# The 80-row token tile of six projections computed in four column groups of TensorE

## The reference

```python
z = jnp.einsum('btd,de->bte', x, w_in)                 # layer 0, w_in (1024, 3588)
hq, hf, hi, hg, fq, fk, fv, ffg = jnp.split(z, [...], axis=-1)   # 512 columns each, ffg 4
o_hg = rms_norm(o_hg, hg_norm_g).reshape(B, T, HG_VO) * jax.nn.sigmoid(hg)
...
y = jnp.einsum('bte,ed->btd', mixed, w_out)            # layer 0, w_out (1024, 1024)
...
y = jnp.einsum('bte,ed->btd', o.reshape(B, T, MLA_HEADS * MLA_V), w_out)   # layer 1
x = layer_norm(ALPHA * x + y, ...)
f = moe(x, router_w, router_bias, w_gate, w_up, w_down)
```

## Time and profile before

| | us |
|---|---|
| median of 3 runs | 1299.97 |
| fastest and slowest run | 1297.56, 1301.29 |
| the profiled execution | 1298.2 |
| its span, first to last instruction | 1296.4 |
| TensorE busy in it | 1138.6 |
| VectorE, ScalarE, GpSimd busy in it | 568.2, 264.4, 218.1 |
| mean granted TensorE clock | 0.954 of full |

### The profile page before, as it was taken

One profiled execution on the slowest core, in us unless ns is written; L12 is line 12 of the kernel. 1 busy time (PEld: TensorE's weight loads), 2 busy tenths in 40 slices (PEclk: granted clock), 3 DMA queues, 4 the chain that ended last, 5 costly groups with the idle time before them and its releaser, 6 DMA issues.

```text
span 1296.4 us, 16787 instructions
## 1 busy us (share of the span) xinstructions
PE 1138.6 (88%) x6345; PEld 611.3 (47%) x6345; DVE 568.2 (44%) x1252; ACT 264.4 (20%) x624; POOL 218.1 (17%) x382
## 2 busy tenths in 40 slices
PE   8999999999799949999639899999999966999965
PEld 4547777643654323333225455676674422333322
DVE  2079879511634335633265230440352353554334
ACT  1214334311410001111002212332330010111112
POOL 0106445322002101001062300000000110100122
PEclk9999999999999959999959999999999987999988
DMA  8113111361842368999662312000105255999843
GB/s 348 65 40 147 74 66 66 110 215 38 67 173 88 119 274 308 379 422 352 247 210 76 133 44 65 2 1 1 66 1 217 70 223 209 339 398 408 284 141 142
DMA packets 41822, 214.71 MB, mean 166 GB/s; under 512 B 4488, under 2 KB 6088, under 8 KB 32400
## 3 DMA queue, kind: packets, MB, share of 16 engines
q1 hardware_dynamic: 24288, 152.57, 30.3%
q0 software_dynamic: 17168, 60.27, 15.2%
q10 hardware_dynamic: 288, 0.80, 0.2%
HBM read 180.31 MB, written 33.29 MB: 165 GB/s over the span
## 4 chain that ended last, share of the span: by engine, by line
PE 76%; DVE 10%; issue 5%; DMA 4%; ACT 3%; POOL 1%; DVEq 0%; SPq 0%; another core or an unknown queue 0%; ACTq 0%; POOLq 0%
PE pair L1420 12%; PE pair L1324 11%; PE pair L1073 11%; PE pair L1441 6%; PE pair L1084 5%; PE pair L1256 5%; PE pair L1190 4%; PE pair L1518 3%; PE pair L1293 3%; PE pair L1570 2%; DMA arena<-x_rows,ints 2%; PE pair L1406 2%; PE pair L1550 2%; PE pair L1291 2%; PE pair L1114 1%
## 5 line engine op out<-in xcount | busy, mean ns | idle before, releaser
L1073 PE MATMUL pair<-ring,xT 128*128 128x512 f32 (+1 forms) x320 | 138.9, 593 | 0.7 <-DMA ring<-in_even_w_in 0.7
L1420 PE MATMUL pair<-ring,arena 128*32 128x512 f32 x608 | 128.5, 595 | 0.0
L1420 PE MATMUL pair<-arena 128*32 128x512 f32 x736 | 104.1, 622 | 7.7 <-issue 4.2
L1073 PEld LDWEIGHTS pair<-ring,xT 128*128 128x128 f32 (+1 forms) x320 | 57.7, 182 | 76.4 <-issue 75.1
L1190 PE MATMUL pair<-xT,ring 128*128 128x296 f32 x320 | 83.4, 415 | 6.1 <-ACT arena L1609 3.0
L843 POOL TENSOR_SCALAR small<-small 128x1 f32<-128x1 f32 (+3 forms) x45 | 16.3, 363 | 422.5 <-DVE small L2114 362.5
L865 POOL TENSOR_TENSOR arena<-arena 128x128 f32<-128x128 f32 x140 | 56.7, 439 | 154.8 <-PE pair L1116 85.6
L1256 PE MATMUL pair<-arena 128*128 128x264 f32 (+5 forms) x280 | 76.5, 402 | 2.6 <-issue 1.4
L2050 DVE TENSOR_REDUCE small<-pair 128x1 f32<-128x144 f32 (+4 forms) x40 | 22.4, 560 | 120.4 <-PE pair L1261 120.2
L1324 PE MATMUL pair<-ring,mixT 128*128 128x512 f32 (+1 forms) x160 | 72.1, 593 | 1.0 <-issue 1.0
L1324 PE MATMUL pair<-ring,xT 128*128 128x512 f32 (+1 forms) x160 | 71.9, 592 | 0.0
(11 more groups left out here) (357 smaller groups left out, 1914.8 us busy)
## 6 DMA issues: line engine op xcount, KB each, us to landing
arena<-in_moe_w_gate_up SPq DMA_DIRECT2D x14, 2048.0 KB, 9.0
ring<-in_moe_w_gate_up SPq DMA_DIRECT2D x12, 2048.0 KB, 9.6
arena<-in_moe_w_down SPq DMA_DIRECT2D x14, 1024.0 KB, 9.6
y_rows<-arena SPq DMA_DIRECT2D x26, 512.0 KB, 8.5
ring<-in_moe_w_down SPq DMA_DIRECT2D x12, 1024.0 KB, 11.5
xT<-in_moe_w_gate_up SPq DMA_DIRECT2D x6, 2048.0 KB, 14.8
ring<-in_even_w_in SPq DMA_DIRECT2D x5, 2048.0 KB, 7.3
y_rows<-xr POOLq DMA_DIRECT2D x12, 512.0 KB, 8.6
```

The lines of the kernel that those rows point to most:

```text
L1073: last = pe.matmul(ps[0:P, 0:n], xT[:, k, 128 * i:128 * i + P], w[:, k, :], start=(k == 0), stop=(k == chunks - 1))
L1420: last = pe.matmul(bank[c, :], xgT[:, e % 2, k, c], expert_place(x)[0][:, k, :], start=(k == 0), stop=(k == KD - 1))
```

## The change

Tile 4 of v, g, fk, fv and of both wo is no longer computed as one block of 80 stationary columns with 512 moving columns. Its rows are cut in three: 0 to 31, 32 to 63 and 64 to 79 (`ROWS`). Each cut goes to the column group whose PSUM partitions are its rows, with the first 384 output columns. The last 128 output columns of all three cuts go one after another to the fourth group, partitions 96 to 127, side by side in the columns where the fourth quarter would have stood (`moved`). For each of eight chunks there are three matmuls of 384 columns and three of 128; the latter run through the eight chunks of the first cut, then of the second, then of the third.

The readers change with it. ScalarE (`token_rows`) reads 80 rows by 384 columns and then three pieces of 128 columns from partitions 96 up, writing each to its own rows. VectorE's residual add of wo tile 4 does the same with both halves in each instruction: 80 rows by 2x384, then three of 2x128. Nothing else changes: not the order, the tickets, the loads, nor the other tiles.

```diff
+        ROWS = [(0, 32), (32, 64), (64, TILES[4])]
+
+        def moved(ps, r, lo=0, n=512):
+
+            a, b = ROWS[r]
+            return ps[96:96 + b - a, lo + n // 4 * r:lo + n // 4 * (r + 1)]
...
+            def last_tile(ps, w, tokens, lo=0):
+
+                K, n = w.shape[1], w.shape[2]
+                m = 3 * n // 4
+                for k in range(K):
+                    for a, b in ROWS:
+                        pe.matmul(ps[a:b, lo:lo + m], tokens(k)[:, a:b], w[:, k, 0:m],
+                                  start=(k == 0), stop=(k == K - 1))
+                    for t in range(3 * k, 3 * k + 3):
+                        r, c = divmod(t, K)
+                        a, b = ROWS[r]
+                        last = pe.matmul(moved(ps, r, lo, n), tokens(c)[:, a:b], w[:, c, m:n],
+                                         start=(c == 0), stop=(c == K - 1))
+                return last
...
+                if i == NT - 1:
+                    last_tile(ps, w, lambda k: xT[:, k, 128 * i:128 * i + P]).then_inc(pe_full.sem(key), 1)
+                    return
...
+                        if i == NT - 1:
+                            last = last_tile(ps, w, lambda k: mixed(k, i), 512 * half)
+                            continue
...
+            def token_rows(f, out, ps, i):
+
+                if i < NT - 1:
+                    return f(out, ps[0:128, 0:512])
+                f(out[:, 0:384], ps[0:TILES[i], 0:384])
+                for r, (a, b) in enumerate(ROWS):
+                    last = f(out[a:b, 384:512], moved(ps, r))
+                return last
...
-                stt(r, xr[0:P, b, :], ALPHA, filled(dve, key)[0:P, :], ALU.mult, ALU.add).then_inc(ps_free.sem(key), 1)
+                ps = filled(dve, key)
+                if i < NT - 1:
+                    added = stt(r, xr[0:P, b, :], ALPHA, ps[0:P, :], ALU.mult, ALU.add)
+                else:
+                    halves = lambda v: v.rearrange("p (h n) -> p h n", h=2)
+                    stt(halves(r)[:, :, 0:384], halves(xr[0:P, b, :])[:, :, 0:384], ALPHA,
+                        halves(ps[0:P, :])[:, :, 0:384], ALU.mult, ALU.add)
+                    for q, (lo, hi) in enumerate(ROWS):
+                        added = stt(halves(rb[lo:hi, b, :])[:, :, 384:512], halves(xr[lo:hi, b, :])[:, :, 384:512], ALPHA,
+                                    halves(ps[96:96 + hi - lo, :])[:, :, 128 * q:128 * q + 128], ALU.mult, ALU.add)
+                added.then_inc(ps_free.sem(key), 1)
```

More of the change, by code:

```diff
@@ L1666, in fk_copy @@
                 P, key = TILES[i], ("fk", i)
-                copy(fks[0:P, i, :], filled(act, key)[0:P, 0:512]).then_inc(ps_free.sem(key), 1)
+                token_rows(copy, fks[0:P, i, :], filled(act, key), i).then_inc(ps_free.sem(key), 1)
             f_exp(0)
@@ L1671, in _ @@
                 P = TILES[i]
-                copy(hv[0:P, i, :], filled(act, ("v", i))[0:P, 0:512]).then_inc(ps_free.sem(("v", i)), 1)
+                token_rows(copy, hv[0:P, i, :], filled(act, ("v", i)), i).then_inc(ps_free.sem(("v", i)), 1)
                 if i == 1:
@@ L1679, in _ @@
                 P, key = TILES[i], ("g", i)
-                act.activation(hgate[0:P, i, :], filled(act, key)[0:P, 0:512], ACT.Exp, scale=-1.0).then_inc(ps_free.sem(key), 1)
+                token_rows(lambda out, ps: act.activation(out, ps, ACT.Exp, scale=-1.0), hgate[0:P, i, :],
+                           filled(act, key), i).then_inc(ps_free.sem(key), 1)
             for u in range(20):
@@ L1721, in _ @@
                     act.wait_ge(*vz_sb["fox"])
-                copy(fv[0:P, i, :], filled(act, key)[0:P, 0:512]).then_inc(ps_free.sem(key), 1)
+                token_rows(copy, fv[0:P, i, :], filled(act, key), i).then_inc(ps_free.sem(key), 1)
             def att_exp(n):
```

## The result

| | before | after |
|---|---|---|
| median of 11 runs, us | 1299.17 | 1288.28 |
| fastest and slowest, us | 1296.48, 1301.29 | 1284.48, 1294.21 |
| ratio of the times | | 0.9922, 95% interval 0.9905 to 0.9939 |
| the profiled execution, us | 1298.2 | 1288.28 |
| its span, us | 1296.4 | 1286.5 |

The change is worth 10.1 us (7.9 to 12.3). The prediction said 7.9 us and 1292.1, with a range of 1288 to 1299: the sign and the mechanism of the block are right, and the time lies at the fast edge of the range.

A forecast was written before the change was run, and what follows sets the result against it. TensorE time was taken to bound the kernel, with all six changed tiles on the chain. 12.7 us saved less 0.5, 0.4, 1.7 and 2.2 leaves 7.9, taking the median from 1299.97 to 1292.1 us; range 1288 to 1299.

The forecast's parts named there:

- The block: Tile 4 of v, g, fk, fv, both wo: 6.87 us falls to 5.28, short passes 0.110 apart, 12.7 us saved.
- In and out of the groups: TensorE around tile 4: 0.09 us to enter, six times (0.5); 0.20 to leave behind v and fk (0.4).
- The readers: ScalarE behind g, fk, fv: 1.16 us for 0.59 (1.7 together); VectorE behind both wo: 2.21 to 2.35 for 1.23 (2.2).
- Loads: Loads waiting for v, g, fk, wo are issued earlier by the saving; g's keeps 8 us of cover under q projection.
- The sum: All places together: 12.7 us saved less 4.8 (0.5 + 0.4 + 1.7 + 2.2) leaves 7.9 us.
- The third rival: Outside the blocks: moved work meets more lower-clock stretches or recurrence gaps, 4 us given back, 1296; chance 0.09.
- the second, slower: Fourth group cannot load weights under its own pass: 0.213 us a pass, block 10.2, 1331.7; decided at 0.131; chance 0.08.
- The first: Fourth group's second matmul waits for first group's second pass at 0.32 us: block 6.08, 1298.5; chance 0.12.
- The fourth: A 16-row cut breaks the grouping, 48 matmuls run one after another: 20.5 us a block, over 100 more; chance 0.01.
- The range: Whole kernel: 1288 to 1299 us to hold 8 in 10, reaching up through the given-back and held-up-group cases.

The follow-up runs named there:

- The repetition: The changed kernel run once more, unaltered, beside the kernel before: 1288.74 us in six runs, ratio 0.9930 (0.9912 to 0.9949).

## Why the prediction was right, step by step

**The block** (5.28 us for 6.87, short passes 0.110 apart) came out as forecast: 0.109 to 0.110. The step that carried it was to read the router's 16 passes in 0.48 us as proof that a load in the same group runs under its pass. The rule of the Trainium skill, "TensorE: Matmul & The Clock Gate", Part 3 under "The mechanism", which has weight loads overlap only where row groups differ, does not hold here: the trace has loads of 97 to 111 ns for the same rows and columns as the running pass, every 0.110 us. The measurement decides.

**In and out of the groups**: 0.09 us to enter at v, g, fk and fv, as taken from the earlier trace rows. To leave costs 0.20 at v, as the earlier trace rows had it: q's first pass starts 0.20 us after the block's last for a spacing of 0.11, and its second 0.35 us later for 0.25. At fk it is contained in the 0.66 of 0.7.

**The readers**: VectorE's 2.29 us lies in the forecast 2.21 to 2.35. ScalarE was undersized: 1.33 and 1.29 for 1.16, since 384 columns cost 0.48 and not the 0.36 that a proportion gave. The profile was to show 0.95 to 1.2. An instruction has a fixed part, which the earlier trace rows showed: 512 columns lasted 0.59 and 128 columns 0.26, not a quarter. That is 0.1 to 0.2 at g and fv each.

**Loads**: here the prediction failed. "g's load keeps its 8 us of cover under the q projection, since both ends move together" held only if the load's own 7.3 us stayed the same. It became 8.4, and with a margin of some 0.5 us that I had not worked out, 0.6 us of v's gain are lost. So g tile 4 ended at 90.6 us and not near 89.8.

**The sum**: 7.9 forecast, 7.65 found in place, 7.04 after g's load. The 3 us beyond that in the measured 10.1 lie outside of the blocks: 1.8 between the statistics and the first experts, and the rest among the attention (3.9 gained), the row from the experts to the latent stage (2.8 lost), the recurrence (1.0 lost) and the last stage (0.9 gained), of the first profiles. The sum had put all these at nothing. The repetition measured 9.1; its interval holds the 7.9 (6.6 to 11.4), and that of the result has it at its very edge. The third rival had looked at the same place with the opposite sign: that moved work meets other transfers and stretches of lower clock and loses. Its mechanism is there: the first profile has 10 us more at 1.2 GHz than the one before, among them the stretch of 3.4 us from 190 us on that costs 1.0 us, and 6.8 us more between 630 and 770 us, in the row from the experts to the latent stage, where TensorE is busy 2.2 us longer. But it does not belong to the change. The three profiles of the kernel before have 120.1, 130.4 and 123.8 us at 1.2 GHz, the two of the changed kernel 130.3 and 120.2.

**Rivals**: the second, slower, is out by 0.110 us against its threshold of 0.131. The first is out for this code; a hold-up of its kind is real for another order of it. The fourth is out: cuts of 16 rows group like those of 32.

**The range** held by 0.3 us, and that is luck: the 7.04 us of the blocks, readers and g's load would have put the time near 1292, and what moved it to the edge was in no term. It was drawn toward the losing side, since everything outside the blocks was taken to be able only to lose. A shift of instructions and transfers has both signs, and the lower end should have been as open as the upper one.

## What to carry to other kernels

Small column groups can be fed several matmuls in a row at full rate (a pass of 128 columns every 0.110 us here), if the code puts each group's instructions near to where they can start; the price is in the readers, whose instructions have fixed parts, and most of it goes away when they read finished pieces under the running block. When a load is said to be hidden, work out by how much: 8 us over a load of 7.3 left 0.5, and 1.1 us more of load used it up. Code that adds instructions to an engine also moves the times at which its program is fetched, and a change of a few us outside of all edited places should be looked for there, and in the granted clock, before it is counted as gain.

## What the hardware showed unexpectedly

- Instruction fetch is visible in time: pieces of 16 KB, one per 256 or so TensorE instructions, stand in the DMA activity beside the data. One inside a 2 MB load went with 8.4 us to landing for 7.3, in five profiles of five; one that came late in some 30 us of transfers issued by GpSimd went with TensorE pauses of 2.0 to 3.0 us.
- TensorE serves a free column group ahead of waiting instructions over a short distance alone: with 48 long passes ahead in the program, the fourth group began when nine were left to start.
- A single stretch of 3.4 us at 1.2 GHz makes a stage visibly longer: TensorE is busy 1.4 us more in the recurrence (215.0 to 216.4 us, the stage 1.0 us longer) and about 2 us more in the experts of layer 1 (178.7 to 178.9 against 180.0 to 180.9). Such stretches come and go between profiles of one kernel.
- The time from the first expert of layer 1 to the end takes 208.8 to 210.5 us in four profiles and 211.7 to 213.7 in ten, of the same kernel too (212.30 and 208.82 for the changed one). The ten have a stretch of 3.4 us at 1.2 GHz among these experts and the four have none, which is some 2 of the 3 us. Three of the four are kernels with tiny matmuls ahead; why is open.
